# A mixture-of-experts router done row tile by row tile, with its overflow places and last tables beside the first expert products

## What is computed

```
h2 = _rmsnorm(x, ffn_norm)                       # 512 rows
group_logits = h2 @ w_rg + b_rg                  # 4 groups, best one taken
expert_logits = h2 @ w_re + b_re                 # 32 experts, 8 in a group
top_v, top_i = lax.top_k(sel, 2)                 # the best two of that group
g2 = softmax(top_v); expert_id = g_idx * 8 + top_i
for e in range(32):
    he = silu(h2 @ w_gate[e]) * (h2 @ w_up[e])   # 1024 -> 256
    y = y + combine[:, e:e+1] * (he @ w_down[e]) # 256 -> 1024
out = _rmsnorm(x + y, final_norm)
```

## Time and profile before

| | |
|---|---|
| median of 3 runs | 1568.11 us (1566.54 to 1569.05) |
| the profiled execution | 1568.56 us, span 1566.8 us |
| mean granted TensorE clock | 0.979 |
| busy: PE, DVE, ACT, POOL | 1481.8, 578.6, 463.2, 324.8 us |
| bytes moved | 233.77 MB |

### The profile page before, as it was taken

The page is one execution under the profiler, slowest core; times in us unless marked ns, Lnnn a source line. Parts: engine busy times, 40 slices in busy tenths (PEclk is TensorE's granted clock), DMA queues, the critical chain, the costliest instruction groups (busy, mean ns, idle before and its releaser), DMA issues.

```text
span 1566.8 us, 17009 instructions
## 1 busy us (share of the span) xinstructions
PE 1481.8 (95%) x6571; PEld 769.0 (49%) x6571; DVE 578.6 (37%) x1113; ACT 463.2 (30%) x955; POOL 324.8 (21%) x351
## 2 busy tenths in 40 slices
PE   5998899999999999999999999999999599999997
PEld 2676554444676454444676444454455433333332
DVE  0164510665644230476554201143155612121225
ACT  1233531221754252221854031232232201011112
POOL 1020100444000120356000000004432133333410
PEclk9999899999999999999999999999999699999999
DMA  9656033331030211211010322111400799999995
GB/s 351 214 211 233 1 108 131 111 108 54 0 112 1 97 54 54 81 54 54 1 55 1 108 69 92 54 54 46 174 1 28 294 372 383 409 374 374 415 411 224
DMA packets 85112, 233.77 MB, mean 149 GB/s; under 512 B 16816, under 2 KB 24758, under 8 KB 70824
## 3 DMA queue, kind: packets, MB, share of 16 engines
q1 hardware_dynamic: 69986, 204.00, 34.6%
q0 software_dynamic: 13824, 24.98, 4.3%
q10 hardware_dynamic: 1222, 3.70, 0.6%
HBM read 266.39 MB, written 16.80 MB: 181 GB/s over the span
## 4 chain that ended last, share of the span: by engine, by line
PE 87%; DVE 4%; ACT 3%; issue 3%; DMA 2%; POOL 1%; SPq 0%; DVEq 0%; POOLq 0%; ACTq 0%
PE PS L1852 17%; PE PS L2279 11%; PE PS L2018 9%; PE PS L2084 7%; PE PS L2305 6%; PE PS L1932 5%; PE PS L1829 4%; PE PS L2082 4%; PE PS L2183 4%; PE PS L1954 3%; PE PS L1942 3%; PE PS L2127 2%; DMA RING<-in_w_mod_dram 1%; PE PS L2154 1%; PE PS L2268 1%
## 5 line engine op out<-in xcount | busy, mean ns | idle before, releaser
L1852 PE MATMUL PS<-RH,RING 128*128 128x512 f32 (+1 forms) x864 | 319.1, 526 | 3.4 <-DMA RING<-in_w_in_dram 3.4
L1852 PEld LDWEIGHTS PS<-RH,RING 128*128 128x128 f32 x864 | 164.0, 192 | 149.6 <-issue 137.2
L2018 PE MATMUL PS<-RING,RY 128*128 128x512 f32 x320 | 139.5, 592 | 0.0
L2279 PE MATMUL PS<-RING,RM 128*64 128x512 f32 x384 | 112.7, 593 | 2.9 <-DVE RM L1680 2.8
L1328 DVE SCALAR_TENSOR_TENSOR RM<-RM,COL 128x512 f32<-128x512 f32 (+1 forms) x180 | 114.2, 704 | 0.1
L2084 PE MATMUL PS<-RH,RING 128*128 128x512 f32 x256 | 114.1, 594 | 0.0
L1369 DVE TENSOR_REDUCE SMALL<-PS 128x1 f32<-128x768 f32 (+1 forms) x80 | 67.7, 846 | 113.0 <-PE PS L1932 113.0
L1932 PE MATMUL PS<-RK,RH 96*128 96x256 f32 (+1 forms) x288 | 106.2, 489 | 1.1 <-ACT WS L1014 0.7
L637 POOL TENSOR_SCALAR SMALL<-SMALL 128x1 f32<-128x1 f32 (+1 forms) x32 | 9.9, 310 | 468.3 <-ACT WS L867 226.7
L2018 PEld LDWEIGHTS PS<-RING,RY 128*128 128x128 f32 x320 | 60.0, 190 | 71.3 <-issue 71.3
L639 POOL TENSOR_TENSOR SMALL<-SMALL 128x1 f32<-128x1 f32 (+2 forms) x54 | 56.5, 1046 | 89.0 <-DVE SMALL L1302 86.4
(11 more groups left out here) (366 smaller groups left out, 2292.6 us busy)
## 6 DMA issues: line engine op xcount, KB each, us to landing
RING<-in_w_in_dram SPq DMA_DIRECT2D x18, 2048.0 KB, 8.0
RING<-in_w_mod_dram SPq DMA_DIRECT2D x12, 2048.0 KB, 9.0
RING<-in_w_expert_gate_dram SPq DMA_DIRECT2D x19, 1024.0 KB
RING<-in_w_expert_up_dram SPq DMA_DIRECT2D x19, 1024.0 KB
RING<-in_w_out_dram SPq DMA_DIRECT2D x8, 2048.0 KB, 8.2
RK<-in_w_expert_down_dram SPq DMA_DIRECT2D x8, 1024.0 KB
X<-in_w_expert_down_dram SPq DMA_DIRECT2D x8, 1024.0 KB
WS<-in_w_expert_down_dram SPq DMA_DIRECT2D x8, 1024.0 KB
```

Of the source, the lines that this page charges most:

```text
L1852: last = mm(o[:, 0:T], w[:, k, m * P:(m + 1) * P], HT[:, k, 0:T], start=(k == 0), stop=(k == 7))
L2018: last = mm(PS[:, j % 2, :], YT[:, k, t * P:(t + 1) * P], w[:, k, :], start=(k == 0), stop=(k == 7))
L2279: last = mm(PS[64 * z:64 * z + 64, n % 2, :], XGT[n % 2][:, k, 64 * z:64 * z + 64], free(GU[n % 3][z], [2048, 2], [1, DE], off=DE * k), st ...
```

## The change

- Router columns are kept with the 32 experts first and the 4 groups last. Experts of other groups are masked (a large number subtracted) and the best two of all 32 taken.
- DVE does the choice per row tile: `choose(n, 0)` and `choose(n, 1)`, and `places(n)` once PE has that tile's ranks. These stand between the residuals and copies of the last output products.
- PE does ranks (`ranks`), expert totals and the places of the main tiles (`main_slots`) per row tile. `output2(15)` is cut in two halves of two products, with `router_logits(2)` and a turn between them; `router_logits(3)` is cut in two.
- Main places no longer pass through the overflow test: `OHM` compares the rank with 0 to 63.
- Overflow places (`overflow_slots`) are summed after the first gate/up product; `overflow_rows()` on DVE stands between `tile_turned(0)` and `tile_turned(1)`, `last_tables()` behind the latter. The tables are turned by `turn_last(z)` behind the second and third gate/up products and copied by ACT.
- The row tile n = 2 is normed by POOL in place of DVE, and ACT stores it after the last mean square, where it was stored before it.
- POOL's later gathers wait for `v_sl` 2. SP's `load_down(1)` waits for `p_sl` 2, and as before for `v_wr` 2, which `last_tables()` now gives.

```diff
             sp.dma_start(GB[:, :], bass.AP(a["final_norm_2"].tensor, 0, [[0, P], [1, D]])).then_inc(d_fw, 16)
-            sp.wait_ge(p_sl, 1)
+            sp.wait_ge(p_sl, 2)
             sp.wait_ge(v_wr, 2)
...
             row_root(5, 2)
+            g.wait_ge(g_rs.sem, g_rs.at(5, 2))
+            g.tensor_scalar(free(XN[:, 1, :], [P, 8], [1, P]), free(X[:, 3, :], [1, 8], [8, P]), rs[:, 1:2], None, ALU.mult).then_inc(g_xn, 1)
...
             g.wait_ge(v_wr, 1)
+            g.wait_ge(v_sl, 2)
             g.wait_ge(m_xt, 1)
             gather(4)
...
             router_rows(2)
-            store_rows(2)
             router_rows(3)
             row_scale(5, (3,))
+            store_rows(2)
...
+                if n < 2:
+                    act.wait_ge(p_la, n + 1)
+                    A(LAST_T[n], PS[:, 7, :], ACT.Copy).then_inc(a_la, 1)
                 copies(n)
...
+                if part == 0:
+                    v.wait_ge(v_l, n + 1)
+                    link(v.max(words(t, 8, 8), seen[:, 32:40]))
+                    link(v.max_index(words(t, 16, 8).bitcast(U32), words(t, 8, 8), seen[:, 32:40]))
+                    link(v.tensor_copy(words(t, 24, 1), words(t, 16, 1).bitcast(U32)))
+                    link(v.tensor_scalar(words(t, 28, 4), IOTA[:, 0:4], words(t, 24, 1), 1.0, ALU.is_equal, ALU.subtract))
+                    link(v.scalar_tensor_tensor(free(masked, [8, 4], [1, 8]), free(words(t, 28, 4), [1, 4], [0, 8]), -NEG,
+                                                free(seen, [8, 4], [1, 8]), ALU.mult, ALU.add))
+                else:
+                    link(v.max(words(t, 40, 8), masked))
+                    link(v.max_index(words(t, 48, 8).bitcast(U32), words(t, 40, 8), masked))
...
+            def places(n, tiles_):
+                t = 3 - n
+                w = 2 * tiles_
+                v.wait_ge(p_rk, n + 1)
...
+            choose(0, 0)
+            choose(0, 1)
             residual2(14)
+            logits(1)
             router_rows(2)
-            logits(1)
-            norm_rows(5, (2,))
...
+            choose(1, 0)
+            choose(1, 1)
+            places(0, 1)
             residual2(15)
+            logits(2)
+            choose(2, 0)
             router_rows(3)
-            logits(2)
+            choose(2, 1)
+            places(1, 1)
             logits(3)
...
+            choose(3, 0)
+            choose(3, 1)
+            places(3, 2)
...
+            v.wait_ge(p_sl, 1)
+            v.tensor_scalar(free(SLOT[:, :], [24, 2], [1, 16]), free(PS[:, 7, :], [16, 2], [1, 16], off=256), float(NONE), None, ALU.add).then_inc(v_sl, 1)
...
+            def overflow_rows():
...
+                v.wait_ge(p_sl, 2)
+                v.tensor_scalar(free(SLOT[:, :], [24, 2], [1, 8], off=16), free(PS[:, 7, :], [8, 2], [1, 8], off=288), float(NONE), None,
+                                ALU.add).then_inc(v_sl, 1)
+
+            def last_tables():
+                v.wait_ge(a_lg, 1)
...
             tile_turned(0)
+            overflow_rows()
             tile_turned(1)
+            last_tables()
...
+            def overflow_slots():
+                pe.wait_ge(v_pos, 4)
+                for j in range(8):
+                    for z in range(2):
+                        last = mm(PS[64 * z:64 * z + 64, 7, 288:304], OHF[:, 64 * j:64 * j + 64], VTF[:, 32 * j + 16 * z:32 * j + 16 * z + 16],
+                                  start=(j == 0), stop=(j == 7))
+                last.then_inc(p_sl, 1)
...
-            output2(15)
+            ranks(0)
+            output2(15, range(2))
+            router_logits(2)
             router_turn(3, 0).then_inc(p_rt, 1)
-            router_logits(2)
+            output2(15, range(2, 4))
+            ranks(1)
+            pe.wait_ge(v_pos, 1)
+            main_slots(0)
+            router_logits(3, range(4))
             router_turn(3, 1).then_inc(p_rt, 1)
-            router_logits(3)
...
+            router_logits(3, range(4, 8))
+            ranks(2)
+            pe.wait_ge(v_pos, 2)
+            main_slots(1)
+            ranks(3)
+            totals()
+            pe.wait_ge(v_pos, 3)
+            main_slots(2)
+            main_slots(3)
...
             turn_tile(1)
+            overflow_slots()
             for n in range(NP):
                 if n + 1 < NP:
                     gate_up(n + 1, range(8) if n + 2 < NP else range(4))
+                if n < 2:
+                    turn_last(n)
                 turn_hidden(n)
```

More of the change, by code:

```diff
@@ L1194, in rows @@
                     A(YO[n % 3][:, 512:1024], PS[:, 3, :], ACT.Copy).then_inc(m_yv, 1)
-            act.wait_ge(p_la, 1)
-            for z in range(2):
-                last = A(LAST_T[z], PS[:, 6 + z, :], ACT.Copy)
-            last.then_inc(a_la, 1)
             half_tile(0)
@@ L1547, in _, with tiles, choose @@
             SUMS = RM[:, 8832:9088]
+            ROUTE, LOGITS, PICK, SCRATCH, EXPS = 8064, 8320, 8576, 9856, 9600
+            SUMS = RM[:, 8832:9088]
+            SCR = RM[:, 9088:9152]
+            ONEHOT = RM[:, PICK:PICK + 256]
+            PRD = RM[:, SCRATCH:SCRATCH + 256]
+            def tiles(base, *dims, off=0):
+                return free(RM[:, base:base + 256], [64, 4], *dims, off=off)
+            words = lambda t, o, n: RM[:, ROUTE + 64 * t + o:ROUTE + 64 * t + o + n]
+            def choose(n, part):
+                t = 3 - n
+                seen = RM[:, LOGITS + 64 * t:LOGITS + 64 * t + 40]
+                masked = RM[:, SCRATCH + 64 * t:SCRATCH + 64 * t + 32]
+                if part == 0:
[9 more added lines that the diff above has]
+                    link(v.max_index(words(t, 48, 8).bitcast(U32), words(t, 40, 8), masked))
+                    link(v.tensor_copy(words(t, 56, 2), words(t, 48, 2).bitcast(U32)))
+                    one = ONEHOT[:, 64 * t:64 * t + 64]
+                    link(v.tensor_tensor(free(one, [32, 2], [1, 32]), free(IOTA, [0, 2], [1, 32]), free(words(t, 56, 2), [1, 2], [0, 32]),
+                                         ALU.is_equal))
+                    own = SUMS[:, 32 * t:32 * t + 32]
+                    last = v.tensor_tensor(own, one[:, 0:32], one[:, 32:64], ALU.add)
+                    if n in (1, 2):
+                        link(last)
+                        before = SUMS[:, 96:128] if n == 1 else SUMS[:, 128:160]
+                        last = v.tensor_tensor(SUMS[:, 96 + 32 * n:128 + 32 * n], before, own, ALU.add)
+                    last.then_inc(v_lg, 1)
+                    for c in range(2):
+                        v.tensor_tensor(free(VTM, [64, 2], [32, 2], [1, 16], off=128 * t + 16 * c), free(one, [32, 2], [1, 2], [2, 16]),
+                                        free(VAL, [1, 2], [0, 2], [0, 16], off=8 * c + 2 * t), ALU.mult)
@@ L1584, in _ @@
-            link(v.tensor_copy(tiles(ROUTE, [1, 4]), tiles(LOGITS, [1, 4])))
-            for t in range(4):
-                last = v.max(words(t, 8, 8), words(t, 0, 8))
-            link(last)
-            for t in range(4):
-                last = v.max_index(words(t, 16, 8).bitcast(U32), words(t, 8, 8), words(t, 0, 8))
-            link(last)
-            link(v.tensor_copy(tiles(ROUTE, [1, 8], off=24), tiles(ROUTE, [1, 8], off=16, dt=U32)))
-            group = free(SCR, [4, 4], [1, 4])
-            link(v.tensor_tensor(group, free(IOTA, [0, 4], [1, 4]), tiles(ROUTE, [0, 4], off=24), ALU.is_equal))
@@ L1595, in _ @@
-            for t in range(4):
-                last = v.tensor_tensor(free(PRD, [8, 4], [1, 8], off=32 * t), free(RM[:, LOGITS:LOGITS + 256], [8, 4], [1, 8], off=64 * t + 4),
-                                       free(SCR, [1, 4], [0, 8], off=4 * t), ALU.mult)
-            link(last)
-            link(v.tensor_reduce(tiles(ROUTE, [1, 8], off=32), free(PRD, [32, 4], [1, 8], [8, 4]), AX, ALU.add))
-            for t in range(4):
-                last = v.max(words(t, 40, 8), words(t, 32, 8))
-            link(last)
@@ L1603, in _ @@
-            for t in range(4):
-                last = v.max_index(words(t, 48, 8).bitcast(U32), words(t, 40, 8), words(t, 32, 8))
-            link(last)
-            link(v.tensor_copy(EID([1, 2]), tiles(ROUTE, [1, 2], off=48, dt=U32)))
-            link(v.scalar_tensor_tensor(EID([1, 2]), tiles(ROUTE, [0, 2], off=24), 8.0, EID([1, 2]), ALU.mult, ALU.add))
-            for k in range(2):
-                last = v.tensor_tensor(free(ONEHOT, [64, 4], [1, 32], off=32 * k), free(IOTA, [0, 4], [1, 32]),
-                                       tiles(ROUTE, [0, 32], off=56 + k), ALU.is_equal)
```

178 lines of the change are left out of this document (90 added, 88 removed).

## The result

The changed kernel takes **1583.32 us** (median of 6 runs, 1581.36 to 1588.67), the kernel before 1566.53 us beside it (6 runs, 1565.88 to 1569.05): ratio 1.0112, 95% interval 1.0100 to 1.0124. The prediction was 1573.1 with a range up to 1580. The direction is right; the loss is more than three times the one forecast, and outside the range.

The account below looks back on a forecast made before the run. PE was busy 95% of the span, the expert stage neck and neck with its weights. PE alone gained 0.5 us, but loads 14.6 us later made D8 +5: profiled 1573.6, median 1573.1 us against 1568.11, range 1564.5 to 1580.

Parts of the forecast that it names:

- D8: Down product of tile 8, at 1367.83 in the kernel before; forecast to start 2.8 to 6.2 us later, +5 taken.
- Rival (3): Before the gathers: stores land before the slots, T is 1241.5, the whole shifts 7.3 us less, 1565.8; chance 0.15.
- Rival (2): Expert tiles 3 to 7: spare in the loads absorbs their lateness, only PE's -0.5 us counts, 1567.6; chance 0.12.
- Rival (4): Before the gathers: stores land late, 1241 or more, T 1251.5, 1575.8; chance 0.48 together with the forecast.
- T: Start of the first expert product, 1252.36 in the kernel before; forecast 1248.8, 3.6 us earlier.
- Rival (1): Weight loads as one line: nothing is overtaken, D8 is late by all of 9.1 us, 1577.2; chance 0.19.
- in full traffic I take all of it: First gather's landing after its issue, beside the weight loads: priced at 6.3 us.
- so I add 0.8 us for part of it at half clock: First expert product after the longer idle: 0.8 us for partly half clock, bounds nothing and 2.7 us.
- The 5.5 us of free time give back that much: DMA engines up to 1302: free time makes up 5.5 of the loads' 14.6 us delay, leaving them 9.1 us late.
- +5 at D8: At tile 8's down product: net loss from late loads, taken a little above the middle of +2.8 to +6.2 us.
- G9: Gate/up product before D8, starting at 1356.07 in the kernel before; 6.7 us of waits forecast up to it.
- After D8 the windows have free time again, and the rest shifts as it is.: Expert stage after D8: DMA windows have free time again (0.71), so no further loss was added.

Follow-up runs that it names:

- e3: Kernel before, with SP's loads held back until the second gate/up product before tile 1's down weights are issued; 1576.32 us, ratio 1.0056.
- e4: Changed kernel with tile 3's gate/up loads issued ahead of tile 1's down load in SP's queue; 1572.37 us, ratio to the kernel before 1.0036.
- e2: Changed kernel with only tile 1's row store put back to its earlier place, before the last turned tile's copy; 1584.00 us, ratio to the kernel before 1.0109.
- e8: Changed kernel, overflow places and tables before the first expert tile, 5 and 4 unread PE products, SP's tile 2 and last-norm loads behind the first turn; 1572.06 us.
- e11: As e8, but 2 unread products behind the overflow places only, tables behind the first turned tile, tile 2's loads issued before the wait for tables; 1569.62 us.
- e13: Changed kernel without the six empty overflow weight transfers of tile 19 and the two waits on them; 1577.77 us, ratio to the kernel before 1.0073.
- e7: Changed kernel with overflow places and tables ahead of the first expert tile, plus 5 and 8 unread PE products during the wait; 1572.58 us, ratio 1.0028.
- e10: Changed kernel with overflow places and tables ahead of the first expert tile, plus 2 and 4 unread PE products during the wait; 1565.87 us, ratio 0.9994.
- e14: e4 with 10 unread PE products between the main slots and the first turn; 1571.14 us, ratio to the kernel before 1.0032.

## Why the prediction was wrong

**Right.** The end of the last output product and the six loads at 1223.84 (predicted 1223.9; the change's own share is 2.85 us and not 2.3, as this execution was 0.6 us early). Main slots at 1235.3 to 1235.5 (1234.6). The last store issued at 1228.95 (1229.1) and landed at 1238.0 (1238.5), so the stores, not the slots, release the gathers; POOL at 1238.98 (1239.5). DMA share near nothing from 1252 to 1270, new waits for weights from the fourth product on, and D8 late. Lateness of the loads as the main cause is shown by e3 (it alone costs the kernel before 8.4 us, half of the 16.8) and by e4 (letting tile 3's loads go first gives back 11 us). Rival (3), on the other side, is out: the stores land at 1238, and e2 shows that their order isn't the reason. Rival (2), spare that absorbs the loads' lateness, is out by e3. Rival (4) had T right (1251.5) but not why: the stores did not land after 1241. Rival (1), no part of the lateness made good, isn't borne out either: by the prediction's own reckoning the loads are 13 us late (below), and D8 starts 9.6 us later.

**Too small, one by one.**
- *"in full traffic I take all of it"*, 6.3 us for the first gather: it took 8.9. The 6.3 was what the kernel before left between issue and use, and I used it as the full price in traffic, while the row of the store beside it, 9.0 us in the same traffic, was the nearer one. Without traffic it is 4.7 to 5.0 (e8, e11). +2.6, and +0.5 for the turn at the lower level. T became 1251.31 instead of 1248.8.
- *"so I add 0.8 us for part of it at half clock"*: +2.6 (9.67 against 7.09). The 12.74 us wait of the changed kernel left the whole first half of the product at the lower level.
- Both stand in the loads' start: T + 18.24 with T 2.5 later, so tile 1's down load came 18.55 us later instead of 14.6.
- *"The 5.5 us of free time give back that much"* and *+5 at D8*. By the same reckoning with 18.55, the loads are some 13 us late at 1302 and not 9.1. D8 starts 9.6 us later, where I had 5: this term is too small by 4.6, and its cause is the lateness above it. PE had waits of 5.8 us up to G9 (predicted 6.7), 1.95 before D8 and 1.7 us of lower clock at tile 3. Some 2.7 us came back by luck, as D8 did not run on the lower clock this time, so that the loss is 7.0 us by the gate/up product behind it. The mechanism held.

**The step that failed: "After D8 the windows have free time again, and the rest shifts as it is."** It does not. At tile 19 the changed kernel waits 6.40 us and loses 2.98 more on the product behind (6.59 and 1.73 in its second trace). These 9.4 us are most of the 12.3 that I missed in the profiled execution; of the 10 missed in the medians e13 puts 4 to 5.6 there. e13 shows that tile 19's empty transfers are what the changed kernel waits for. Why they land after 24 us in its traces, and within the 17.6 us that PE gives them in the kernel before and in e2, stays open: neither the time between issue and use nor the lateness of the loads decides it. I had no term for such a wait in the prediction.

The table gives an estimate of the same sum in one line: 0.30 of DMA share in 50 us are 15 us of idle engines, and at 0.7 that is some 10 us, where I had 5; the wait at tile 19 comes on top.

## What to carry to other kernels

Where a stage runs level with its loads, what counts in the stage ahead of it is how long the DMA engines stand idle, not how soon the compute engine starts; before moving work behind a start, look which load instruction waits for that work, and let loads that don't need it go first (one edit in SP's list, e4, gave back 11 of 17 us). Where the loads fill the queues, list how long each late transfer is given between its issue and its use, and compare that with the landing times seen in the same traffic: tile 19 gives 17.6 us, and such transfers took 12 to 25. Look at more than one trace before a wait is put down to a change: this one was missing in e2 and came in e7. And price a latency by the nearest transfer in the same traffic, not by the slack that an old schedule happened to leave.

## What the runs showed of the hardware

- An indirect transfer whose rows all lie out of bounds, and which moves no weights, is not free to wait for: behind full queues it was reported landed 24.0 and 25.5 us after its issue (changed kernel, e11), the one of tile 19 after 12.1 to 14.2 us in three other kernels (e10, e8, e11). In the first of these stretches POOL's queue moved 907 packets with 1.84 MB and SP's 1086 with 7.96 MB, and 698 of all packets were under 512 bytes. The Trainium skill (DMA: Bandwidth & Descriptors, Queues, rings and completion order) says that each DMA engine takes turns between its queues packet by packet; small packets that wait a turn beside large ones fit these counts, but no run here separates that from the length of POOL's own queue.
- The same gather of 128 rows took 4.7 to 5.0 us to land with the queues nearly idle and 8.9 to 10.1 beside loads.
- A scaling of 128x1024 by POOL took 3.86 us here (I had 3.1 from 128x512 rows); it was hidden.
- After the changed kernel's waits PE ran at the 1.2 GHz level: after 12.74 us eight turns took 1.97 us instead of 1.04 to 1.10, and the first product 1.06 us a pair for 5.2 us; after 4.19 us the product of tile 3 took 8.78 us instead of 7.09. Products without a use put in the long wait (e10) brought the 2.4 GHz level back: the granted clock was 0.50 from 1234 to 1244 and 1.00 from 1246 to 1250, and the first product took 7.09 us. In e14 it was 1.00 from 1238 to 1246 and 0.50 from 1248 to 1250, behind two idle times of 1.71 and 1.38 us with a turn between them.
